# Two layers of a three-stage transformer kernel: the layer loop written out, and the last norm, its squares and the store taken tile by tile

## What is computed

```python
def second_block(x, mem, ...):
    for l in range(DEPTH_2):                      # DEPTH_2 = 2
        h = rmsnorm(x, norm_mix[l])
        ...                                       # delta rule, top-k attention
        o_xa = memory_branch(xq, rmsnorm(mem, norm_mem[l]), w_mem_kv[l])
        ...
        x = x + merged @ w_out[l]
        h = rmsnorm(x, norm_ffn[l])
        gt, up = jnp.split(h @ w_ffn_in[l], 2, axis=-1)
        x = x + (jax.nn.silu(gt) * up) @ w_ffn_out[l]
    return rmsnorm(x, norm_final)
```

## Time and profile before

| | us |
|---|---|
| three runs: median | 2740.78 |
| lowest, highest | 2740.01, 2741.67 |
| the profiled execution's own time | 2743.33 |
| its span, first to last instruction | 2741.5 |
| PE busy in it | 2594.0 (95%) |
| DVE, ACT, POOL busy | 1890.0, 1519.4, 180.4 |

### The profile page before, as it was taken

One profiled execution on the slowest core, in us unless ns is written; L12 is line 12 of the kernel. 1 busy time (PEld: TensorE's weight loads), 2 busy tenths in 40 slices (PEclk: granted clock), 3 DMA queues, 4 the chain that ended last, 5 costly groups with the idle time before them and its releaser, 6 DMA issues.

```text
span 2741.5 us, 44045 instructions
## 1 busy us (share of the span) xinstructions
PE 2594.0 (95%) x16251; PEld 2169.4 (79%) x16251; DVE 1890.0 (69%) x2149; ACT 1519.4 (55%) x1543; POOL 180.4 (7%) x211
## 2 busy tenths in 40 slices
PE   5999998999999999999999999999999999999997
PEld 4756887777777777778898788799798977887995
DVE  3444767999999999986668665655466786756553
ACT  3433546787887878874545554443345554534432
POOL 0000010000000000000046000000000650000000
PEclk9999998999999999999999999999999999999998
DMA  7434537999999999984344115445444440254545
GB/s 280 173 134 183 209 123 298 385 391 382 391 384 383 390 381 394 385 343 139 146 154 154 63 71 200 176 178 185 171 161 154 154 154 33 89 211 169 185 154 192
DMA packets 79658, 610.09 MB, mean 223 GB/s; under 512 B 16004, under 2 KB 21700, under 8 KB 24968
## 3 DMA queue, kind: packets, MB, share of 16 engines
q1 hardware_dynamic: 79496, 607.87, 58.2%
HBM read 606.79 MB, written 1.05 MB: 222 GB/s over the span
## 4 chain that ended last, share of the span: by engine, by line
issue 45%; PE 36%; DVE 7%; POOL 6%; ACT 3%; DMA 2%; SPq 1%; POOLq 0%; ACTq 0%; DVEq 0%
PE psum_scalar L1799 5%; PE psum_scalar L1800 5%; PE psum_vector L550 3%; PE psum_vector L552 3%; PE psum_vector L551 3%; POOL arena L3537 2%; DVE weight_slabs_rounded L1757 2%; PE psum_scalar L577 2%; ACT arena_rounded L1746 2%; PE psum_scalar L550 2%; PE psum_scalar L552 2%; PE psum_scalar L551 2%; PE psum_vector L1771 2%; POOL arena L3540 2%; DMA weight_slabs<-in_mixer_slabs 1%
## 5 line engine op out<-in xcount | busy, mean ns | idle before, releaser
L2196 DVE TENSOR_TENSOR weight_slabs_rounded<-weight_slabs,arena_rounded 128x2048 fp32r<-128x2048 f32 x208 | 477.9, 2307 | 348.3 <-ACT arena_rounded L2193 299.7
L2193 ACT ACTIVATE arena_rounded<-weight_slabs 128x2048 fp32r<-128x2048 f32 x208 | 396.3, 1913 | 361.6 <-PE psum_vector L552 227.9
L550 PE MATMUL psum_scalar<-arena_rounded,arena_rounded 128*128 128x256 f32 (+1 forms) x1456 | 472.7, 325 | 23.4 <-DVE weight_slabs_rounded L2196 9.7
L550 PE MATMUL psum_vector<-arena_rounded,arena_rounded 128*128 128x512 f32 (+3 forms) x1264 | 456.1, 361 | 14.9 <-DVE weight_slabs_rounded L2196 14.8
L1757 DVE TENSOR_TENSOR weight_slabs_rounded<-weight_slabs,arena_rounded 128x2048 fp32r<-128x2048 f32 x192 | 431.2, 2287 | 20.8 <-ACT arena_rounded L1746 13.3
L1746 ACT ACTIVATE arena_rounded<-weight_slabs 128x2048 fp32r<-128x2048 f32 x192 | 362.2, 1910 | 51.8 <-PE psum_scalar L1800 23.1
L552 PE MATMUL psum_vector<-arena_rounded,arena_rounded 128*128 128x512 f32 (+1 forms) x896 | 348.0, 388 | 0.0
L551 PE MATMUL psum_vector<-weight_slabs_rounded,arena_rounded 128*128 128x512 f32 x880 | 343.6, 390 | 0.0
L1799 PE MATMUL psum_scalar<-arena_rounded,arena_rounded 128*128 128x512 f32 x768 | 310.0, 404 | 19.7 <-DVE weight_slabs_rounded L1757 11.8
L550 PEld LDWEIGHTS psum_scalar<-arena_rounded,arena_rounded 128*128 128x128 f32 x1456 | 279.4, 192 | 56.2 <-issue 24.5
L551 PE MATMUL psum_scalar<-arena_rounded,arena_rounded 128*128 128x256 f32 x992 | 281.3, 284 | 0.0
(11 more groups left out here) (497 smaller groups left out, 4176.3 us busy)
## 6 DMA issues: line engine op xcount, KB each, us to landing
weight_slabs<-in_layer_slabs SPq DMA_DIRECT2D x103, 2048.0 KB, 7.8
weight_slabs<-in_expert_slabs SPq DMA_DIRECT2D x192, 1024.0 KB, 8.1
arena<-in_expert_slabs SPq DMA_DIRECT2D x96, 1024.0 KB, 7.9
weight_slabs<-in_mixer_slabs SPq DMA_DIRECT2D x32, 2048.0 KB, 8.4
weight_slabs<-in_layer_slabs SPq DMA_DIRECT2D x6, 1024.0 KB, 5.4
arena<-in_mem SPq DMA_DIRECT2D x3, 1024.0 KB, 12.0
arena<-in_b_gate SPq DMA_DIRECT2D x6, 512.0 KB, 8.2
arena<-in_x SPq DMA_DIRECT2D x1, 1024.0 KB, 4.9
```

Source lines behind the costliest of these rows:

```text
L550: pe.matmul(out, left[0], right[0], start=start, stop=False)
L2193: e.activation(fr(high), low, ACT.Copy).then_inc(S("weights_high"), 1)
L2196: e.tensor_tensor(fr(low), low, fr(high).bitcast(F32), ALU.subtract).then_inc(S("weights_split"), 1)
```

## The change

It does six things.

1. The loops are plain Python loops: each engine's program holds the body twice, and every semaphore value is a constant.
2. In the second copy, what prepares a third layer is left out on every engine: the slabs, the memory rows, their squares, root, transposes and gains, and the two splits.
3. The gains of the last norm get another room (from 72 to 96 of the arena) and are loaded beside slab 37 of the second layer, where the memory rows were.
4. In the last pair of k of both layers' down projection PE does tile 0 for both k and then tile 1.
5. In the second layer DVE reports x after each tile's sums, and ACT squares each tile at its report.
6. The last multiplication reports each tile, and each tile is stored by its own DMA.

```diff
@@ half_spent
-            name, per_layer, value = lay_spent[g]
-            if g < 0:
-                value = value - per_layer
-            e.wait_ge(parts["lay"][name], per_layer * l + value)
+            name, value = lay_spent[LH * l + g]
+            e.wait_ge(parts["lay"][name], value)
@@ sp_layers
-            with sp.Fori(0, 2) as l:
+            for l in range(2):
...
-                    if n == LS - 2:
+                    if n == LS - 2 and l == 0:
                         next_layer(0)
...
                     if kind == "ffn" and at == BANK:
-                        sp.dma_start(mem_rows, a["mem_2"][0].rearrange("(t p) d -> p t d", p=P)).then_inc(S("mem_in"), 16)
-                next_layer(1)
-                next_layer(2)
-            sp.wait_ge(S("layer_free"), 3)
-            sp.dma_start(nfin, a["norm_final_2"].partition_broadcast(P)).then_inc(S("final_gain_in"), 16)
-            sp.wait_ge(S("layer_free"), 4)
-            sp.dma_start(out.rearrange("(t p) d -> p t d", p=P), x).then_inc(S("stored"), 16)
-            sp.wait_ge(S("stored"), 16)
+                        if l == 0:
+                            sp.dma_start(mem_rows, a["mem_2"][0].rearrange("(t p) d -> p t d", p=P)).then_inc(S("mem_in"), 16)
+                        else:
+                            sp.dma_start(nfin, a["norm_final_2"].partition_broadcast(P)).then_inc(S("final_gain_in"), 16)
+                if l == 0:
+                    next_layer(1)
+                    next_layer(2)
+            for t in range(NT):
+                sp.wait_ge(S("layer_free"), 3 + t)
+                sp.dma_start(out[t * P:(t + 1) * P, :], x[:, t, :]).then_inc(S("stored"), 16)
+            sp.wait_ge(S("stored"), 32)
@@ pe_layers
-                    if n == 3:
-                        pe.wait_ge(S("memn_ready"), l + 2)
+                    if n == 3 and l == 0:
+                        pe.wait_ge(S("memn_ready"), 2)
                         memory_to_T(0)
-                    if n == 4:
+                    if n == 4 and l == 0:
                         memory_to_T(4)
...
-                for k in range(FC):
-                    if k % 4 == 0:
-                        pe.wait_ge(S("ff_split"), 6 * l + k // 4 + 1)
-                    if k % 2 == 0:
-                        w = half()
-                    for t in range(NT):
+                for pair in range(0, FC, 2):
+                    if pair % 4 == 0:
+                        pe.wait_ge(S("ff_split"), 6 * l + pair // 4 + 1)
+                    w = half()
+                    rows_first = pair == FC - 2
+                    for k, t in [(pair + (i % 2 if rows_first else i // 2), i // 2 if rows_first else i % 2) for i in range(4)]:
@@ act_layers
-                Splitter(e, l + 1, high=True).upto(1)
+                if l == 0:
+                    Splitter(e, 1, high=True).upto(1)
...
-            e.wait_ge(S("x_ready"), 7)
-            squares(pre, x, xsq)
+            for t in range(NT):
+                e.wait_ge(S("x_ready"), 7 + t)
+                pre.go(e.activation(xsq[:, t, :], x[:, t, :], ACT.Square, accum_out=ss[:, t:t + 1]))
+            pre.sync()
+            e.sem_inc(S("squares"), 1)
@@ vec_layers
-                    if n == 2:
+                    if n == 2 and l == 0:
                         over_rms(mem_rows, mem_rows, 3, 5, "memn_ready")
-                    if n in (3, 4):
+                    if n in (3, 4) and l == 0:
                         memory_gains(4 * (n - 3))
...
-                Splitter(e, l + 1, high=False).upto(1)
+                if l == 0:
+                    Splitter(e, 1, high=False).upto(1)
                 for t in range(NT):
                     for half in range(2):
                         cols = slice(half * BANK, (half + 1) * BANK)
                         V.give(tt(x[:, t, cols], x[:, t, cols], V.take(), ALU.add))
-                V.given()
-                e.sem_inc(S("x_ready"), 1)
-                e.sem_inc(S("layer_free"), 1)
+                    if l == 1:
+                        V.given()
+                        e.sem_inc(S("x_ready"), 1)
...
             for t in range(NT):
-                pre.go(stt(x[:, t, :], x[:, t, :], rstd[:, t:t + 1], nfin, ALU.mult, ALU.mult))
-            pre.sync()
-            e.sem_inc(S("layer_free"), 1)
+                stt(x[:, t, :], x[:, t, :], rstd[:, t:t + 1], nfin, ALU.mult, ALU.mult).then_inc(S("layer_free"), 1)
```

More of the change, by code:

```diff
@@ L2081, in build @@
         xsq = room(56, NT, D)
-        nfin = room(72, D)
+        nfin = room(96, D)
         FEW = 88
@@ L2190, in upto @@
                         before = half_before(g)
-                        if before is not None and (before >= 0 or not isinstance(self.l, int)):
+                        if before is not None and LH * self.l + before >= 0:
                             half_spent(e, self.l, before)
@@ L2789, in squares @@
                 e.sem_inc(S("squares"), 1)
-            with e.Fori(0, 2) as l:
+            for l in range(2):
                 A = Banks(e, psa, m["scalar_full"], m["scalar_free"], base=LAY_A * l, looped=True)
@@ L3069, in act_layers @@
                         feed_forward_high(n - 1)
-                    if n == 1:
-                        e.wait_ge(S("mem_in"), 16 * l + 32)
+                    if n == 1 and l == 0:
+                        e.wait_ge(S("mem_in"), 32)
                         squares(step, mem_rows, xsq)
@@ L3504, in vec_layers @@
                         V.give(tt(x[:, t, cols], x[:, t, cols], V.take(), ALU.add))
[L3505 to L3510 removed]
+                    if l == 1:
+                        V.given()
+                        e.sem_inc(S("x_ready"), 1)
+                if l == 0:
+                    V.given()
+                    e.sem_inc(S("x_ready"), 1)
+                    e.sem_inc(S("layer_free"), 1)
+                assert V.n == LAY_V - 4 * l and (l == 1 or step.n == LAY_DVE), (V.n, step.n)
+            e.wait_ge(S("squares"), ROOTS_SO_FAR + 6)
+            root(pre, ROOTS_SO_FAR + 9, 2, D)
             e.wait_ge(S("final_gain_in"), 32)
             for t in range(NT):
[L3513 to L3515 removed]
+                stt(x[:, t, :], x[:, t, :], rstd[:, t:t + 1], nfin, ALU.mult, ALU.mult).then_inc(S("layer_free"), 1)
         def pool_layers(e, pre):
```

26 lines of the change are left out of this document (12 added, 14 removed).

## The result

The changed kernel took 2723.08 us (median of four runs, 2721.38 to 2723.38) beside 2740.4 for the kernel before on the same chip: 0.9935 of its time, with a 95% interval from 0.9923 to 0.9947. That is 17.3 us less. A second set of runs gave 2721.46 beside 2743.15, a ratio of 0.992 (0.9905 to 0.9936). A single execution of either kernel lies up to 8 us from its median, so the two profiled ones, whose spans are 21.9 us apart, overstate the change a little.

A forecast was written before the change was run, and what follows sets the result against it. PE was taken to bound the layers, with a chain without PE at the end. Turn 2.4, transposes 1.6, slabs 0, end 9.5 and registers 4.0 make 17.5 us: 2740.8 - 17.5 = 2723.3 us, range 2716 to 2730.

The forecast's parts named there:

- The turn, 2.4: Between the two layers: PE's 2.46 us of idle time at the loop's branch goes; 2.4 us, from 0 to 2.5.
- The transposes, 1.6: Layer two, two places: eight transposes for a third layer cost PE 0.79 us at each; leaving them out saves 1.6 us.
- The slabs, 0: A third layer's slab issued ahead of slab 51: leaving it out saves 0 us, between 0 and 1.6.
- The end, 9.5: Behind T, the end of PE's last product: 18.5 us become 9.0, saving 9.5 us, between 8.4 and 10.4.
- rival 3: At the end, the two stores go one behind the other: T + 11.1, 2.1 us less gained, 2725.4 us; chance 0.12.
- Registers, 4: Both layers: without register operations, DVE's gaps and changes of engine shrink; 2 us a layer, 4 us, from 0 to 12.
- Rival 1: Both layers: registers count for more, 12 us at the upper bound giving 2715; range 2711 to 2718 us, chance 0.12.
- Rival 2: Another wait takes back the gains of turn and registers; 11.1 us remain, 2729.7, from 2729 to 2733; chance 0.12.
- Rival 4: PE's straight code in the layers stops at 88 instruction packets; at 0.3 us each 26.4 us, 2749.7; chance 0.02.
- Rival 5: The end stays held by the gains' DMA or a DVE wait; 8.7 us gained or less, 2732; chance 0.04.

The follow-up runs named there:

- filled kernel before: The kernel before with products of a constant put into four of PE's long waits (factors and slab 47, both layers), not layer one's entry: 2731.37 us, ratio 0.9971.
- filled kernels: Kernels with constant products in PE's long waits: the kernel before 2731.37 us, that with only its loops written out 2719.75, the changed kernel 2708.58.
- filled pair: With constant products in PE's waits, the kernel before (2731.37 us) beside, for PE's stops, loops written out alone (2719.75), or, for the whole change, the changed kernel (2708.58).
- unfilled pair: Without constant products in PE's waits: the kernel before, 2740.51 us, beside the same with only its loops written out, 2731.12 us, ratio 0.9963.
- filled changed kernel: The changed kernel with 13 or 14 constant products put into each of PE's five longest waits, layer one's entry included: 2708.58 us, ratio 0.9889.
- half filled: The changed kernel with half as many constant products (7, 7 and 6) in the same five waits of PE: 2715.59 us, ratio 0.9908.

## Why the prediction was right, and where its parts were off

It said 2723.3 us, from 2716 to 2730; the median is 2723.08. By its parts:

- **The turn, 2.4.** Right: the stop of 2.46 is gone in every kernel with written-out loops. A second price showed up only in the filled kernel before: behind its stop of 2.55 us the clock fell too, which cost 1.7 us. In the trace of the forecast it did not.

```profile
1972.00:1976.00 4.00, 1.70 (x13) 1.71 (x14) 3.06 (x5) 0.79 (x1) 0.00 (x0) 0.95 0.96 358
1976.00:1980.00 4.00, 4.00 (x24) 4.00 (x24) 0.00 (x0) 1.13 (x1) 0.00 (x0) 0.62 0.72 298
```

- **The transposes, 1.6.** Right. From the middle norm's last sum to the up projection's last product on DVE, layer two takes 136.1 us in both filled kernels with transposes and 134.3 in the one without.
- **The slabs, 0.** Right within its bounds: the wait at slab 51 is 1.23 us instead of 1.67, and over the filled kernels it scatters from 1.32 to 2.56.
- **The end, 9.5.** The chain behind T was right to 0.2 us: T + 8.8 against T + 9.0, with the gains at T + 3.1. The stores overlap, against rival 3; the span ends 3.2 us behind the issue of the second, and one store of 1 MB was 1.2 us slower. The Trainium skill (SBUF — State Buffer, "The DMA setup-cost knee") advises to join DMA-bound transfers into the largest one. For this last store, which waits for DVE tile by tile, two came out ahead. What was off is the other side of the subtraction. The 18.5 was one execution's, with a landing of 7.8 us for the gains; over five it is 16.2 to 18.5, and the term is 7.4 to 9.7, mostly about 7.8. The earlier trace rows had it in sight: DVE waits there 5.58 us for a DMA, and SP had issued a slab for the third layer just ahead.
- **Registers, 4.** Wrong in place, and too small: some 6.7 us by the pieces above. The step that failed is that the gaps of 0.23 us on DVE shrink towards 0.05 and take half of the convolutions' waits with them, 1.2 us a layer. They shrank to 0.15, the splits ran 0.07 longer, and the waits gave 0.06. The other part, 0.8 a layer, was too small: a change of engine in the delta rule lost 0.11 to 0.15 us in most places, not 0.05 to 0.1, and the stretch with the 64 x 64 products became 2 us shorter on average. PE's stops show less of it and scatter more: other than turn and entry they are 6.1 us shorter in the filled pair (21.8 - 15.2 less 3.2 for the filled entry is 3.4; 19.5 - 14.3 less 2.5 for the turn is 2.7), 4.2 of it in and beside the 64 x 64 products, and 2.6 in the unfilled pair.
- **Rival 1** (registers more, 2711 to 2718) had the direction right, 6.7 us for 4, but neither its 12 nor its time was measured. **Rival 2** (taken back by another wait) fell: no new wait appeared at the turn. **Rival 4** (stops in straight code) fell: PE has in the changed kernel's layer two a single unexplained stop of 0.82 besides the wait for slab 47, where it had two and the turn's before, and the instruction queue brought 103 packets instead of 108. **Rival 5** fell with the end.

Added up from these sizes the change is 2.5 + 1.7 + 7.8 + 6.7 = 18.7 us, plus what the clock makes of it: 21.1 in the filled pair, 17.3 and 21.7 in the two unfilled sets. So an end that was 1.7 too large and registers 2.7 too small largely cancelled, and the forecast was nearer than its parts. That it lies 0.2 us from the first median is luck: the second set of runs is 1.6 us away from the first, and 4.4 further below the kernel before beside it. The clock as a source of time did not stand in it at all, though the page of the kernel before had it in view: a mean granted clock of 0.984, where each 0.001 over the two layers' 1490 us is up to 1.5 us.

What stays open: why the clock falls behind a given stop in one execution and not in another, and what the stops without releaser in the 64 x 64 products are. They vary between executions of one program (in layer one of the changed kernel PE's stretch with them took 40.8 and 41.0 us, in layer two 39.5 and 40.5 less the lost clock) and more between kernels: none in layer two of the filled changed kernel, one of 1.9 us in the half filled one. No run here took them apart.

## What to carry to other kernels

A loop of two passes whose tail prepares a third one costs more than its branch: its last loads stand in front of what the end really needs, and its last splits stand in front of the last sums. Look at what a transfer's landing in the trace had ahead of it before taking it for a constant, and at more than one execution where a term of the sum hangs on a single landing. And where PE waits for some microseconds on a chain of other engines, put harmless products into the wait: that was worth 8 to 13 us here, about half of what the whole change brought or more.

## What the runs showed of the hardware that was not expected

- The granted clock fell behind PE's stops of very different length, and not always. In the filled changed kernel PE stood for 1.80 us ahead of 1507.41 in layer one, and the clock fell:

```profile
1504.00:1508.00 4.00, 2.20 (x15) 1.57 (x13) 3.11 (x10) 3.46 (x12) 0.00 (x0) 1.00 0.47 135
1508.00:1512.00 4.00, 3.69 (x13) 3.06 (x13) 3.32 (x8) 1.82 (x4) 0.00 (x0) 0.57 0.92 391
```

  In the half filled kernel it stood for 1.81 at the same place, and the clock stayed. That kernel's layers have both of these, behind stops of 2.16 us (up to 1769.26) and of 1.47 us (up to 2240.36):

```profile
1769.00:1773.00 4.00, 3.74 (x33) 3.74 (x34) 2.66 (x7) 2.24 (x2) 0.00 (x0) 1.00 1.05 451
2240.00:2244.00 4.00, 3.33 (x14) 2.68 (x15) 3.59 (x12) 2.38 (x6) 0.00 (x0) 0.73 0.88 360
```

  The clock stayed behind the longer one and fell behind the shorter. So no length of a stop alone foretells it in these traces.
- Products of a constant by itself, whose bank nobody reads, keep the clock up like real ones. 14 of them take 3.29 us, and the wait for the factors ended as far behind the last real product as without them (3.7 us).
- Two stores of 512 KB on one queue overlap: issued 1.2 us apart, they landed 2.6 and 2.7 us behind their own issues.
- A load of 512 KB landed in 3.3 us with the DMA engines free and in 5.4 to 7.8 us behind a slab of 2 MB on the same queue. In its early place beside other slabs it took 10.7 to 13.9.
